# Ten more weight slots per late layer as seven block products, and attention values two heads at a time

## The reference, cut to what matters

```python
for l in range(2):                                   # the late layers
    h = rms_norm(x, mix_pre_g[l])
    proj = h @ w_in[l]                               # cq 384, ckv 256, kr 32, z 512, dq 256, dk 256, dv 256
    out_a = mla_group(cq, ckv, kr, ...)              # 8 heads: softmax(q k^T) @ v, v of 64 columns each
    out_b = sgu_group(z, ...)
    out_c = diff_group(dq, dk, dv, ...)              # 4 heads, two softmaxes each
    mix = concat([out_a, out_b, out_c]) @ w_mix_out[l]          # 1024 x 1024
    x = x + rms_norm(mix, mix_post_g[l])
    h = rms_norm(x, mem_pre_g[l])
    q = h @ mem_w_q[l]                               # 1024 x 1024, 4 heads of 256
    o = softmax(q k^T) @ v                           # k, v from a memory of 256 tokens
    x = x + rms_norm(o @ mem_w_o[l], mem_post_g[l])  # 1024 x 1024
    h = rms_norm(x, ffn_pre_g[l])
    x = x + rms_norm(conv_ffn(h, ...), ffn_post_g[l])
```

## Time and profile before

| | |
|---|---|
| runs | 1825.63, 1828.3, 1831.82 us, median 1828.3 |
| profiled execution | 1828.68 us, of which the span of the trace 1827.0 |
| mean granted TensorE clock | 0.991 of 2.4 GHz |
| TensorE matmuls busy | 1764.7 us, 97% |
| VectorE busy | 703.0 us, 38% |
| ScalarE busy | 426.2 us, 23% |
| late layers | from 803 us to the end |

### The profile page before, as it was taken

The page is one execution under the profiler, slowest core; times in us unless marked ns, Lnnn a source line. Parts: engine busy times, 40 slices in busy tenths (PEclk is TensorE's granted clock), DMA queues, the critical chain, the costliest instruction groups (busy, mean ns, idle before and its releaser), DMA issues.

```text
span 1827.0 us, 27748 instructions
## 1 busy us (share of the span) xinstructions
PE 1764.7 (97%) x11486; PEld 1411.8 (77%) x11486; DVE 703.0 (38%) x1589; ACT 426.2 (23%) x930; POOL 63.3 (3%) x60
## 2 busy tenths in 40 slices
PE   7999999999999999999899999999999999999997
PEld 4776788656666666678678889999887688899996
DVE  4778434111111111132521216665434312176664
ACT  3642321000000100021632221111214522311112
POOL 1021001000000000010000100000000000000000
PEclk9898999999999999999999999999999999999999
DMA  9111574999999999954223334444443133244420
GB/s 397 62 56 62 216 300 177 383 423 422 422 422 422 422 422 422 422 212 151 102 73 136 115 116 150 167 163 166 140 144 138 47 139 115 93 142 160 166 88 23
DMA packets 53658, 383.44 MB, mean 210 GB/s; under 512 B 6080, under 2 KB 6336, under 8 KB 7360
## 3 DMA queue, kind: packets, MB, share of 16 engines
q1 hardware_dynamic: 52272, 376.91, 52.9%
q10 hardware_dynamic: 1296, 5.24, 0.7%
HBM read 381.08 MB, written 1.05 MB: 209 GB/s over the span
## 4 chain that ended last, share of the span: by engine, by line
PE 87%; DVE 9%; ACT 2%; DMA 1%; issue 1%; SPq 0%; POOLq 0%; DVEq 0%; ACTq 0%
PE ps L598 83%; DVE arena L2106 2%; PE ps L596 2%; DVE arena L2100 2%; DVE ring L2100 1%; DMA ring<-in_stream 1%; PE ps L655 1%; DVE small L2610 0%; DVE arena L2103 0%; DVE ring L2106 0%; DVE ring L2258 0%; DVE arena L2508 0%; ACT arena L1967 0%; ACT arena L1959 0%; DVE small L2100 0%
## 5 line engine op out<-in xcount | busy, mean ns | idle before, releaser
L598 PE MATMUL ps<-arena,ring 128*128 128x256 f32 (+2 forms) x3360 | 664.9, 356 | 9.8 <-DVE arena L2100 2.1
L598 PEld LDWEIGHTS ps<-arena,ring 128*128 128x128 f32 x3360 | 557.5, 192 | 96.4 <-issue 37.3
L598 PE MATMUL ps<-ring,arena 128*64 128x256 f32 (+4 forms) x3168 | 481.1, 417 | 0.0
L598 PEld LDWEIGHTS ps<-ring,arena 128*64 128x64 f32 (+1 forms) x3168 | 291.4, 147 | 173.1 <-issue 84.4
L598 PE MATMUL ps<-arena 128*128 128x128 f32 (+4 forms) x2538 | 350.0, 297 | 5.3 <-ACT arena L1959 1.7
L598 PEld LDWEIGHTS ps<-arena 128*128 128x128 f32 (+2 forms) x2538 | 312.2, 190 | 35.0 <-issue 19.2
L2100 DVE TENSOR_TENSOR arena<-arena,ps 128x256 f32<-128x256 f32 (+2 forms) x176 | 69.4, 413 | 206.8 <-ACT arena L1856 202.7
L2106 DVE SCALAR_TENSOR_TENSOR arena<-arena,par 128x255 f32<-128x255 f32 (+1 forms) x282 | 125.7, 488 | 6.5 <-ACT arena L2076 2.3
L598 PE MATMUL ps<-ring 128*128 128x256 f32 (+2 forms) x896 | 115.2, 295 | 4.0 <-issue 2.2
L598 PEld LDWEIGHTS ps<-ring 128*128 128x128 f32 (+2 forms) x896 | 97.6, 157 | 17.3 <-issue 4.5
L2508 DVE RECIPROCAL arena<-arena 128x256 f32<-128x256 f32 x13 | 22.8, 1753 | 205.0 <-ACT arena L1586 205.0
(11 more groups left out here) (194 smaller groups left out, 1016.2 us busy)
## 6 DMA issues: line engine op xcount, KB each, us to landing
ring<-in_stream SPq DMA_DIRECT2D x358, 1024.0 KB, 9.9
arena<-in_xc ACTq DMA_DIRECT2D x1, 1024.0 KB, 6.0
xT<-in_xc ACTq DMA_DIRECT2D x1, 1024.0 KB, 10.5
arena<-in_mem ACTq DMA_DIRECT2D x1, 1024.0 KB, 4.8
out_y<-xT ACTq DMA_DIRECT2D x2, 512.0 KB, 3.1
ring<-in_dft ACTq DMA_DIRECT2D x1, 512.0 KB, 8.0
arena<-in_sguw ACTq DMA_DIRECT2D x2, 256.0 KB, 2.6
row<-in_row SPq DMA_DIRECT2D x1, 474.0 KB, 24.9
```

The source lines that it names most:

```text
L598: i = nc.tensor.matmul(out, lhsT, rhs, start=start, stop=stop, skip_group_check=skip)
```

## The change

In each late layer ten slots get the seven-product form: slot 1 of the mixing input, dq, dk and dv, slots 1 and 2 of both output projections, and slots 1 and 2 of the memory query. The form is taken out of `up` into `seven`, which waits for the weight sums once, ahead of the third product. `flip` makes the tokens stationary. VectorE gets the token sums (one set for each of the four inputs), the weight sums and the joins of these slots in its program; ScalarE no longer copies them out but waits for the join (`cb_ok`) where it reads the result. The MLA heads' `values` is done for two heads at once, their matmuls in turn, every second head; the transposed probabilities get four buffers instead of two.

```diff
-        PTb = [A(17728, TT, T), A(18240, TT, T)]
+        PTb = [A(at, TT, T) for at in (17728, 18240, 19264, 19776)]
...
+            def seven(b, s, src, hsum, wsum, ready, done, flip=False):
+                a11, a12, a21, a22 = blocks(ring[:, s % SLOTS, :])
+                def product(r, wt, mov, inc=None):
+                    for c in range(4):
+                        one, two = (mov, wt) if flip else (wt, mov)
+                        mm(products(b)[:, r, :], one[:, c, :], two[:, c, :], c == 0, c == 3, inc if c == 3 else None)
+                product(0, a11, src[:, 0:4, 0:P])
+                product(1, a12, src[:, 4:8, 0:P])
+                pe.wait_ge(wsum_ok, ready)
+                product(4, a22, hsum[:, 3])
+                product(5, wsum[:, 0], hsum[:, 0])
+                product(2, wsum[:, 1], hsum[:, 1])
+                product(6, wsum[:, 2], hsum[:, 2])
+                product(3, wsum[:, 3], src[:, 4:8, P:T], done)
...                                                    # out_proj
+                    if n in (1, 2):
+                        seven((5, 2)[n - 1], s, src, hs, ws[n - 1], sums_at(l, ("mix", "mem")[o], n + 1), y_sum)
...                                                    # mixing input
+                    if k == 1:
+                        seven(4, s, h, hs2, ws[0], sums_at(l, "win", 2), y_sum)
...
-                    late_b(s, h, range(TT), 0, T)
+                    if k < 3:
+                        if k:
+                            pe.wait_ge(cb_ok, joins_at(l, "win", k))
+                        seven((6, 4, 6)[k], s, h, hs2, ws[(1, 0, 1)[k]], sums_at(l, "win", 3 + k), y_sum, True)
...                                                    # values
+                    if 4 <= u < 12:
+                        for kt in range(TT):
+                            for j in range(2):
+                                mm(bank(2, T)[64 * j:64 * j + 64, :], vt[:, kt, (u + j - 4) * 64:(u + j - 4) * 64 + 64],
+                                   PTb[(u + j) % 4][:, kt, :], kt == 0, kt == 1, inc=o2_ps if kt and j else None)
...
-                    if u > 4:
-                        values(u - 1)
-                values(11)
+                    if u > 4 and u % 2 == 0:
+                        values(u - 2)
+                values(10)
...                                                    # memory query
+                    if k in (1, 2):
+                        if k == 2:
+                            pe.wait_ge(late_ev, ljobs[0])
+                        seven((6, 0)[k - 1], s, h, hs2, wq[k - 1], sums_at(l, "q", k + 1), y_sum)
+                    else:
+                        if k:
+                            pe.wait_ge(cb_ok, joins_at(l, "q", 2))
...                                                    # ScalarE, y_squares
+                    joined = n in (1, 2) and m % 3 < 2
+                    out = cb[:, 0, 2 * n - 2:2 * n, :] if joined else bank(4 + n, 2, T)
...                                                    # VectorE
                 scaled(h, n0, PR(f"mix_pre{l}"), hc_ok)
+                token_sums(h, hs2)
+                weight_sums(win_slot(l) + 1, ws[0])
+                weight_sums(win_slot(l) + 3, ws[1])
+                join_in(0)
+                weight_sums(win_slot(l) + 4, ws[0])
+                join_in(1)
+                weight_sums(win_slot(l) + 5, ws[1])
                 small_rstd(rs)
...                                                    # cq and ckv scaled, then
+                join_in(2)
+                join_in(3)
...                                                    # rotations, layer norm, heads; then
+                dve.wait_ge(o2_ev, 12 * l + 8)
+                out_sums(cat, 0)
                 add_scaled(yb, n0 + 1, 3 * l)
                 scaled(h, n0 + 2, PR(f"mem_pre{l}"), hc_ok)
+                token_sums(h, hs2)
+                for k in (1, 2):
+                    weight_sums(out_slot(l, 1) - 4 + k, wq[k - 1])
                 for u in range(12, 16):
+                    if u < 14:
+                        dve.wait_ge(y_sum, y_at(l, "q", u - 11))
+                        join((6, 0)[u - 12], ...)
                     maxima(u)
                     normalize(u)
+                dve.wait_ge(o2_ev, 12 * l + 12)
+                out_sums(cat2, 1)
```

More of the change, by code:

```diff
@@ L43 @@
 UP_SUMS = 2 * (FFN_PAIRS - 1)
+W_SUMS, SUMS_AT = UP_SUMS + 15, {"win": 0, "mix": 5, "q": 8, "mem": 11, "ffn": 14}
+W_JOINS, JOINS_AT = UP_SUMS + 10, {"win": 0, "mix": 4, "q": 6, "mem": 8, "ffn": 10}
+Y_SUMS, Y_AT = 18, {"win": 0, "mix": 4, "q": 8, "mem": 10, "ffn": 14}
 KV_START, KV_HEADS, KV_GAP = 4, (8, 4), (1, 2, 1)
@@ L395, in blocks, with products, sums_at, joins_at @@
             return v[:, 0, 0:4], v[:, 0, 4:8], v[:, 1, 0:4], v[:, 1, 4:8]
-        def products(w):
-            return bank(2 * w, 8, P)
+        def products(b):
+            return bank(b, 8, P)
+        hs2 = A(6656, 4, 4, P)
+        wq = [A(10752, 4, 4, P), A(2048, 4, 4, P)]
+        def sums_at(l, part, n):
+            return W_SUMS * l + SUMS_AT[part] + n
+        def joins_at(l, part, n):
+            return W_JOINS * l + JOINS_AT[part] + n
+        def y_at(l, part, n):
+            return Y_SUMS * l + Y_AT[part] + n
+        def win_slot(l):
+            return out_slot(l, 0) - 9 - (KV_HEADS[l] + 4) // 2
+        def out_slot(l, k):
+            return up_slot(l, 0) - (14, 4)[k] - (2 if l + 1 < LAYERS else 0)
         def up_slot(l, i):
@@ L1448, in _ @@
                     s = arrive()
-                    for half in range(2):
-                        late_a(s, half, h, h0 + 8 if k == 0 and half == 0 else None)
+                    if k in (1, 2):
+                        if k == 2:
+                            pe.wait_ge(late_ev, ljobs[0])
+                        seven((6, 0)[k - 1], s, h, hs2, wq[k - 1], sums_at(l, "q", k + 1), y_sum)
+                    else:
+                        if k:
+                            pe.wait_ge(cb_ok, joins_at(l, "q", 2))
+                        for half in range(2):
+                            late_a(s, half, h, h0 + 8 if k == 0 and half == 0 else None)
                     release()
@@ L1502, in up @@
                             pe.wait_ge(conv2_ok, FFN_PAIRS * l + 1)
[L1503 to L1521, removed]
+                        seven(2 * w, s, h, hs, ws[w], sums_at(l, "ffn", 2 * (i - 1) + w + 2), up_ps)
                         release()
@@ L1929, in _ @@
                 act.dma_start(sguw, sguw_d[l]).then_inc(ld_sgu, 16)
-                for j in range(5):
+                for j in (0, 1, 4):
                     b = late_take()
@@ L1935, in _ @@
                 act.wait_ge(late_ev, ljobs[0] - 1)
+                act.wait_ge(cb_ok, joins_at(l, "win", 1))
                 A_(sq[:, 0:5, :], cv, ACT.Square).then_inc(cq_ok, 1)
[L1937 to L1943, removed]
+                act.wait_ge(cs_ps, l + 1)
+                root(rs[:, 0:T], bank(3, T), 384)
+                root(rs[:, T:2 * T], bank(3, 2 * T)[:, T:2 * T], 256).then_inc(sm_ok, 1)
                 b = late_take()
@@ new lines, in halves, with join @@
+                def halves(v):
+                    return v.rearrange("p (a t) -> p a t", a=2)
+                def join(b, low, high, w):
+                    m = products(b)
+                    two = [P, 2, P]
+                    u = halves(ub[:, w])
+                    link(V.tensor_copy(first_p[:, w], m[:, 0, :]))
+                    link(tt(low, over(first_p[:, w], two), m[:, 1:3, :], ADD))
+                    link(tt(u, over(low[:, 1], two), m[:, 5:7, :], ADD))
+                    tt(low[:, 1], u[:, 0], m[:, 3, :], ADD)
+                    tt(high, over(u[:, 1], two), m[:, 4:6, :], ADD).then_inc(cb_ok, 1)
@@ L2717, in side_taps @@
                     signal(ins, conv2_ok, False)
-                token_sums()
-                weight_sums(1, 0)
-                weight_sums(1, 1)
+                dve.wait_ge(hc_ok, 24 * l + 24)
+                token_sums(h)
+                for w in range(2):
+                    weight_sums(up_slot(l, 1) + w, ws[w])
                 for i in range(FFN_PAIRS):
```

152 lines of the change are left out of this document (85 added, 67 removed).

## The result

The changed kernel takes 1802.1 us (median of four runs, 1799.7 to 1804.8) against 1828.1 us (1825.6 to 1831.8) before; ratio 0.9856, interval 0.9834 to 0.9879. In five more runs on another occasion it took 1802.9 us (1799.7 to 1805.5) against 1827.4 us (twelve runs, 1819.0 to 1831.4), ratio 0.9866, interval 0.9844 to 0.9889. The forecast of 1806.5 us had the sign and most of the size; the time lies 1.4 us under the range.

A forecast was written before the change was run, and what follows sets the result against it. TensorE's instructions were taken to bound the kernel. Slots 13.2 plus values 9.2, less 0.3 and 0.3, gave 21.8 us off 1828.7, so 1806.9, and 1806.5 us for the median; range 1803.5 to 1813.5.

The forecast's parts named there:

- What bounds the kernel: Whole kernel: bound by the number and size of TensorE's instructions, not their clock; TensorE busy for 97% of the span.
- The slots: Ten slots in each of two late layers go from 6.91 to 6.25 us, saving 13.2 us of TensorE time.
- half of the eighth that the form saves: Seven-product slots: half the saved eighth is lost, as a 128-column record costs a little more than half a 256-column one.
- The values: MLA heads: a pair's `values` overlaps in two column groups, costing one head's 1.0 us; 9.2 us saved in both layers.
- the 0.3 us for head 11: Layer 1's MLA loop: 0.3 us may be lost as head 11's transposes wait for VectorE's normalization.
- `out_proj` of the mix in layer 0: Sign of being right: this projection starts about 7.2 us earlier, at 952.5.
- VectorE hidden: Late layers: VectorE's added 114 us of sums and joins is in total free, being busy for 38% of the span.
- just-in-time places: Inputs where VectorE's sums or joins are ready barely before TensorE asks: a loss of 0.3 us in sum, bounds 0 and 3.
- TensorE's waits before `L598`: Sign of being right: TensorE's idle time there in the late layers doesn't grow by more than 1 us.
- The rival in which VectorE becomes the bound: First sums of each input: additions take twice as long, TensorE waits 30 us in eight inputs, time 1837 us; chance 3%.
- The sum: Whole kernel: 13.2 + 9.2 - 0.3 - 0.3 = 21.8 us off the profiled execution's 1828.7, giving 1806.9 us.

The follow-up runs named there:

- slots alone: The changed kernel with the MLA heads' `values` done one head at a time: 1812.3 us, ratio 0.9914, net stage 987.7 us.
- the pair in the same columns: The changed kernel with both heads of a pair writing partitions 0 to 63, in one column group, copied out by two ScalarE copies: 1809.5 us.
- head after head: The changed kernel with both matmuls of a pair's first head ahead of those of the second, column groups as before: 1806.9 us, one execution.
- the kernel with 29 us more of TensorE waits: The changed kernel with VectorE making the token and weight sums of the ten new slots of a layer twice: 1847.3 us.

## Why the prediction was right or wrong

- **What bounds the kernel:** right. The gain is what TensorE's own instructions lose, and all stages without an edit between the start of the late layers and the last projection kept their length to 0.01 us.
- **The slots:** 13.2 us forecast, 13.0 measured (slots alone, and stage by stage). 0.112 us per record held for the flipped slots too. One reading beside the sum was wrong: not half of the eighth that the form saves is lost to the shorter records, but a quarter (7/8 of 6.91 is 6.05 us, the slot takes 6.25).
- **The values:** the mechanism was right, shown by the pair in the same columns (+6.8 us) and by the timeline; the term was too small. With the 0.3 us for head 11 taken off, 8.9 us were forecast; measured were 10.0 alone and 9.9 in the stages. I priced a head at 1.0 us from the end of the loop, where nothing follows closely; between other work it costs 1.11, its change of shape included, as the kernel before already showed (921.70 to 923.68, less 0.87 for `scores`). `out_proj` of the mix in layer 0 started at 948.1 us where 952.5 was forecast; 3.8 of these 4.4 us lie ahead of the change. The overlap is not tied to the order of the matmuls in the program.
- **Head 11 in layer 1:** its wait grew by 0.38 us, the 0.3 us of the estimate.
- **VectorE hidden:** right, and the loss of 0.3 us for just-in-time places did not come. At the query of layer 0 slot 3 starts behind the transposes with no idle time, and the first sums, slowed by GpSimd as forecast, are ready just in time. In the late layers TensorE's waits before `L598` (`L628` in the changed kernel) came to 12.2 us in place of 13.2. The rival in which VectorE becomes the bound had the price of sums twice as long right, 30 us, of which 29 were measured; its whole time of 1837 us was too low by 10, as it left out the half-clock time that came with such waits.
- **The sum:** 21.8 us forecast for what were 22.9 in the changed stages. The values with head 11 gave 1.0 more, the slots 0.2 less, and the 0.3 us for just-in-time places stayed away.
- **What failed** is the step from the sum to a time and its range: "The median of the runs is 0.4 us under the profiled one, so 1806.5 us", with 3 us of room below. The miss of 4.4 us has three parts, beside 0.2 us in the median of before. The terms of the sum were 1.1 us too small, nearly all of it the values term. The end of the kernel was put at nothing without a reason: it got 1.0 us shorter by the place of an instruction fetch, which no row that I read shows. These two lead from the 1828.1 us of before to 1804.2, which lies in the range. The last 2.1 us are spread, for which the range left no room, as it held only the unknown costs of the edits. Half-clock time that goes from 17.1 us (changed) over 27.3 us (before) to 30.7 us (head after head, the same net stage as changed), half of it lost, moves single executions by 5 us and more.
- **Is the surplus only spread?** The first comparison's 26.0 us and the second's 24.5 lie above the 22.9 + 1.0 = 23.9 us that the stages show, and both intervals contain 23.9. The mean granted clock of the executions settles it. If the part (1 - clock) x span is taken off each time, 23 executions of the kernel before average 1811.3 us and nine of the changed one 1787.5: 23.8 us apart, with a standard error of 0.3. So the surplus lies in the clock, of which the changed kernel's executions lost 1.2 us less on average. Whether that is chance or the change isn't shown.

## What to carry to other kernels

In this kernel matmuls whose outputs lie in different column groups ran at the same time even though each alone fills all rows: two 64-column products issued together cost 1.11 us, as much as one. So look for such products that stand apart and issue them together. A seven-product form pays by the record's time at the smaller width (6.25 against 6.91 us here, not 7/8), and needs a plain slot ahead of it as cover for the sums; work out for each input when the sums are ready and when they are asked for, since each us of lateness was paid here, and half-clock time came with it. Where single executions differ by half-clock stretches, compare a stage's length with these stretches taken out: that told 0.3 us apart here, where medians of whole times left 2 us open, and a forecast's range has to include them.

## What the runs showed of the hardware that was not expected

- An 8 KB instruction fetch of VectorE beside the last 512 KB output transfer delayed the end by 1.0 us (landing 3.1 against 2.6 us by the median of both transfers); 64 instructions more in VectorE's program moved it away.
- Executions of one kernel differ in how long the granted clock is at its half: up to the last projection 23.9 us in two traces of the kernel before and 27.3 us in a third; it was 64.8 us in the kernel with 29 us more of TensorE waits.
- Two heads' matmuls issued one head after the other overlap as well as in turn (1.99 against 1.98 us with scores): the second head's records start 0.013 us beside the first head's.
